# Two chunks of merge logits multiplied in the neighbourhood attention's block instead of the scan's

## The reference

```python
h = concatenate([h_ctx, h_lat])
(na_q, na_k, na_v, na_gate, pool_u, pool_gate, rw_r, rw_k, rw_v, rw_gate,
 rw_lw, rw_la, merge_logits) = split(h @ w_in, IN_SPLIT_POINTS)
y_na   = neighbourhood_attention(...)      # 16 heads of 64, softmax with bias and mask
y_pool = multiscale_pool(...)
y_rw   = rwkv_readout(... wkv_scan in both directions, 16 heads of 64 ...)
g_na, g_pool, g_rw = split(sigmoid(merge_logits), 3)
merged = g_na * (b_na @ w_branch[0]) + g_pool * (b_pool @ w_branch[1]) + g_rw * (b_rw @ w_branch[2])
out = merged @ w_out
```

## Time and profile before

| | us |
|---|---|
| median of 3 runs | 4159.89 |
| these runs | 4159.89, 4160.18, 4151.89 |
| the profiled execution, its own time | 4156.79 |
| its span | 4155.0 |
| TensorE busy in the span | 3791.7 (91%) |
| `att_h`, first to last matmul | 2657.3 to about 2811 |
| `feat`, first and last start of a dense product | 2818.7 and 3106.6 |
| `scan`, first to last start of a unit | 3121.4 to 3785.6 |
| `tail`, first start of a dense product to the span's end | 3797.6 to 4155.0 |

### The profile page before, as it was taken

How to read it: one execution, slowest core, us unless ns; L and a number is a source line. 1 busy time by engine, 2 the same in 40 slices (tenths; PEclk the granted TensorE clock), 3 DMA queues, 4 the chain that set the end, 5 groups by cost and what they waited for, 6 DMA issues and landing times. The chain is left out here.

```text
span 4155.0 us, 59251 instructions
## 1 busy us (share of the span) xinstructions
PE 3791.7 (91%) x25005; PEld 1903.5 (46%) x25005; DVE 1508.2 (36%) x2754; ACT 662.2 (16%) x1351; POOL 579.4 (14%) x840
## 2 busy tenths in 40 slices
PE   8899996899759999997999999898988899888998
PEld 1354443345424444453444444453435666664443
DVE  0499995372212214222100013243543334332411
ACT  0100001103230010231100000142441222221000
POOL 0001101111100001110000012341112323322100
PEclk9899998999979999998999999999999999999999
DMA  8788996872365456435545578636763334334662
GB/s 292 285 297 294 337 329 220 278 246 93 139 238 180 162 192 226 136 113 222 181 165 173 165 256 305 213 115 228 252 230 116 105 109 127 110 102 152 210 227 101
DMA packets 360590, 822.68 MB, mean 198 GB/s; under 512 B 27604, under 2 KB 63724, under 8 KB 353396
## 3 DMA queue, kind: packets, MB, share of 16 engines
q1 hardware_dynamic: 258524, 485.10, 35.1%
q0 software_dynamic: 73632, 275.55, 18.5%
q10 hardware_dynamic: 28172, 58.27, 3.7%
HBM read 698.02 MB, written 120.82 MB: 197 GB/s over the span
## 5 line engine op out<-in xcount | busy, mean ns | idle before, releaser
L1058 PE MATMUL gemm_a_g_ps<-store_w,turned 128*128 128x512 f32 (+1 forms) x1152 | 454.8, 557 | 2.4 <-PEq L205 2.4
L835 DVE SCALAR_TENSOR_TENSOR pmods_acc<-pmods_w,cond,pmods_acc 128x512 f32<-128x512 f32 x600 | 424.2, 748 | 23.9 <-issue 0.9
L1058 PE MATMUL out_c_g_ps<-store_w,turned 128*128 128x512 f32 (+1 forms) x1024 | 399.3, 552 | 0.0
L1058 PEld LDWEIGHTS gemm_a_g_ps<-store_w,turned 128*128 128x128 f32 x1152 | 208.5, 190 | 248.2 <-issue 248.2
L2305 PE MATMUL scan_g_ps<-store_w,turned 64*64 64x512 f32 x2048 | 295.4, 612 | 19.9 <-PEq L1441 14.2
L1058 PEld LDWEIGHTS out_c_g_ps<-store_w,turned 128*128 128x128 f32 x1024 | 184.5, 190 | 213.8 <-issue 213.8
L1058 PE MATMUL att_a_g_ps<-store_w,turned 128*128 128x512 f32 x512 | 238.3, 598 | 13.8 <-PEq L3130 9.9
L1058 PE MATMUL gemm_hq_g_ps<-store_w,turned 128*128 128x512 f32 x512 | 222.1, 597 | 7.4 <-PEq L3130 7.4
L1058 PE MATMUL out_a_g_ps<-store_w,turned 128*128 128x512 f32 x512 | 220.3, 592 | 1.1 <-PEq L205 1.1
L1058 PE MATMUL out_a_g_ps<-store_w,turned_c 128*128 128x512 f32 x512 | 220.2, 592 | 0.0
L1058 PE MATMUL feat_g_ps<-store_w,turned 128*128 128x512 f32 x384 | 182.6, 625 | 21.6 <-ACT feat_stage L1688 13.6
(11 more groups left out here) (439 smaller groups left out, 4983.6 us busy)
## 6 DMA issues: line engine op xcount, KB each, us to landing
store_w<-in_w_in SPq DMA_DIRECT2D x160, 1024.0 KB, 5.5
pmods_w<-in_w_mod POOLq DMA_DIRECT2D x40, 2048.0 KB, 11.4
store_w<-in_a_w_in SPq DMA_DIRECT2D x48, 1024.0 KB, 9.0
store_w<-in_c_w_in SPq DMA_DIRECT2D x48, 1024.0 KB, 5.2
mods_w<-in_w_mod SPq DMA_DIRECT2D x32, 1024.0 KB, 9.4
store_w<-in_a_w_out SPq DMA_DIRECT2D x32, 1024.0 KB, 5.0
scan_raw<-s_feat SPq DMA_DIRECT2D x112, 256.0 KB, 4.1
s_feat<-feat_o POOLq DMA_DIRECT2D x16, 1536.0 KB, 8.8
```

The lines of the kernel that those rows point to most:

```text
L835: v.scalar_tensor_tensor(a, src, x, a, ALU.mult, ALU.add)
L1058: mm = pe.matmul(to, lhs, self.store.slot[i % self.store.NS][:, k, :width], start=first, stop=last)
```

## The change

`merge_early` becomes chunks 0 to 3, and `merge_late` chunks 4 to 7, 10 and 11. Nothing else differs.

```diff
-        merge_early, merge_late, merge_last = merge_chunks(0, 2), merge_chunks(2, 8) + merge_chunks(10, 12), merge_chunks(8, 10)
+        merge_early, merge_late, merge_last = merge_chunks(0, 4), merge_chunks(4, 8) + merge_chunks(10, 12), merge_chunks(8, 10)
```

## The result

The changed kernel takes **4196.24 us** (median of 4 runs, 4193.17 to 4197.16) against 4160.03 of the kernel before beside it: a ratio of 1.0084, 95% interval 1.0068 to 1.0099. That is 36 us more and outside the predicted range. The profiled execution took 4196.41 us, with a span of 4194.6.

What follows compares the result with a forecast made beforehand. TensorE was taken to bound `att_h`, while scan stages wait for DVE, ACT or POOL, partly covered by units. `att_h` 47.5 us longer less scan 31 shorter gave +16.5 on 4156.8, stated as 4174 us; range 4162 to 4188.

Steps and rivals of the forecast that it cites:

- The evictions: `att_h`: four more evictions on ACT, each with two table loads, taken as 1 us for all.
- the 50 units priced at 0.88: `att_h`: new units standing where PE doesn't wait, 0.88 us each, 44.0 us longer.
- Rival 2: `att_h` has room: each unit costs 0.05 us, 3 us in all; change ends at -28, 4129. Chance 0.01.
- A: Scan: 12 units out behind half stages, 0.63 us each, 7.6 us back.
- B: Scan: 12 units out behind level stages, 0.37 us each, 4.4 us back.
- C: Scan: units behind stages ending in one short DVE or ACT operation, 0.60 us back each.
- D: Scan: units behind further stages ending in one short DVE or ACT operation, 0.60 us back each.
- E: Scan: 8 units out behind av of latent rounds, 0.87 us each, 7.0 us back.
- F: Scan: units behind other stages ending in one short DVE or ACT operation, 0.60 us each, 2.4 us back.
- G: Scan: 16 units at places where they hide entirely, 0.14 us each, 2.2 us back.
- rival 4: Scan: PE idler, time at 1.2 GHz doubles, 10 to 13 us lost; net +28, 4185. Chance 0.12.
- Rival 3: Scan: fewer matmuls mean fewer unexplained PE stalls, up to 10 us more back; net +6, 4163. Chance 0.18.

Runs made afterwards that it cites:

- none_at_halves: Changed kernel, but scan units placed as in the kernel before, less the 64 behind half1 to half5 and latent level5: 4179.32 us, ratio 1.0053.
- att_plus_two: Kernel before with chunks 2 and 3 multiplied a second time in `att_h`, its scan unchanged: 4221.75 us.
- scan_without_two: Kernel before with the products of chunks 2 and 3 left out of the scan, `att_h` as before: 4155.36 us in one run.
- none_between: Changed kernel, but scan units placed as in the kernel before, less the 64 behind turned, tz, outer, chain1 and y: 4171.75 us, ratio 1.0023.
- none_at_levels: Changed kernel, but scan units placed as in the kernel before, less the 64 behind level1 to level4 and context level5: 4185.48 us, ratio 1.0065.
- scan_one_chunk: Kernel before with only one of the scan's eight chunks multiplied, seven left out: 4042.34 us in one run.
- placed_192: Changed kernel with the scan's units placed by a table: two behind products, one behind av or rk and level1 to level4, rest spread: 4178.52 us, ratio 1.0042.
- placed_256: Kernel before with the scan's units placed by a table: two behind products, one behind av or rk and level1 to level4, rest spread: 4154.73 us, ratio 0.999.

## Why the prediction was wrong

**att_h: the total right, with luck.** 47.4 us for 47.5. The ten waits at L1982 are gone and the start-up wait shrank by 1.7, as forecast; that the block was bound by TensorE, read from starts without gaps, held. But two terms were off and cancelled. The evictions, for which I took 1 us, brought five waits of 4.2 us at L1996. That leaves 43.2 us for the 64 units, not 46.5: the 50 units priced at 0.88 cost about 0.81 each, as the step of 5.66 us for 4.04 shows. A row gives the distance to the next start, and another unit in the same step did not add the whole of it. Rival 2, room in `att_h`, is out: PE's weight loads are busy 52% there, and by the rule that was weighed the block would have had room; measured was 0.74 us a unit. Where there was room is below 64 units.

**scan: wrong, 6.7 us for 31.** Two steps failed. (`feat`, forecast unchanged within 3 us, was 3.8 shorter; nothing was tried there.)

The first is the group table, above all *A* and *B*. "12 x 0.63 = 7.6" and "12 x 0.37 = 4.4": the halves gave 2.0 and the levels 3.4 in the chain, together 5.4 for 12.0: the 0.37 that a bare level gives back is taken by the half behind it. The single prices were right (0.63 in none_at_halves, 0.37 at 3275.03). Wrong was to add them as if places were independent. I measured a stage from its start to the next stage's and did not ask what the next one then does. The sign of it stood in the earlier trace rows: the half behind the bare level has x16 and a wait for L2675 in front, where the others have x32 and no break. C and D, at 7.3 for 7.2, were right, and E, at 6.7 for 7.0, taken by itself. But F gave -1.3 for 2.4, and part of that is the same error. Of the chain stages chain1 lost 8 of its 16 units and gave back only 1.2 us: a chain1 of a context round with its unit takes 2.07 us where `outer` ahead of it has none, and 1.61 where it has one. And chain2 got 4 units more, for 3.0 us, which a price per unit of the group can't show. G gave 1.0 for 2.2, and the wait for L2766 grew as I said, to 5.0 us. In all the chain gave 19.2 us for 30.8.

The second is that I took every us of chain for a us of scan. 12 went into excess. Part of it goes with what rival 4 describes: time at half clock rose from 21 to 50 us (the rounded 0.98 had made me start from 27), and of the 14 us that half of that would be, some 8 show in places without a gap. Rival 3 took the stalls for something that fewer matmuls would lessen; they did not fall, 13 of 24.4 us before and 13 of 26.0 after. How much of the 12 us belongs to the change is open. The same scan in another kernel had 11 us more excess with 256 units (att_plus_two, 61.4 for 50.2) and 1 more with 192 (scan_without_two, 63.5 for 62.2), so that in the mean of both pairs 7 us went there. That shorter stages bring more of it is borne out by none_at_halves and none_between (68.8 and 70.1), not by none_at_levels (42.3) and scan_one_chunk (40.0); placed_192 and placed_256 say less, since 14.5 and 6.9 us of their growth are waits for DVE's addition. Gaps, clock and chance can't be parted further, since no run held the clock and changed the gaps, or the reverse.

**Sign, range, chances.** The forecast's sign held, and with it the reason: TensorE full in `att_h`, waits under the units in the scan. Its size did not: +36 for +14. The condition under which I called it wrong ("if the scan shrinks by under 20") was met. The range ended where rival 4's ended; rival 4 and the failed group sum together, 47.5 - 19 + 12 = 40, were in no case of mine. I had priced the bad cases one at a time.

## What to carry to other kernels

Before a filler's price is taken from two like stages, read on through the next stage: with two interleaved chains a filler behind one stage may only be using up the wait of the next. Price a removal over the pair, or over the round. And a unit that fills waits has its worth at a corner: in `att_h` the second 32 cost 0.10 us each and each one beyond them 0.74, while without any the engine's clock fell and the block took nearly as long as with 128.

A filler that can itself wait belongs where its wait is over: two units in a row behind `products` met an addition that DVE does later in its own order, and held up all of TensorE's work for up to 3.8 us.

Where a sum comes out to a tenth of a us, check its terms all the same: in `att_h` two errors of 3 us cancelled.

Where stages are made shorter, don't count on all of it: in six of the eight kernels with a shorter chain than before's and no more units, the changed one among them, 45 to 94% of what the chain gained was lost again to excess. With single profiles whose excess differs by up to 11 us for the same scan, that is a tendency and not a price.

## What I had not expected of the hardware

- TensorE stops in the middle of a run of short matmuls for 1.0 to 3.2 us from start to start, each time until 1.2 to 1.65 us after one of its instruction packets of 16 KB landed, 26 of 26 in two traces. The views call it "issue".
- Half of the stretches at 1.2 GHz in the changed scan (6 of 12) begin within 1.5 us of the end of such a gap of 1.8 to 2.5 us.
- Without its filling units `att_h` ran at 1.2 GHz for some 160 of its 195 us, though PE was busy in 76% of it (148.58 of 195).
- A unit on the whole array between 64x64 products costs 0.37 us more behind a level and 0.06 more behind a half than one on quadrants, with a quarter of its instructions. Why the two differ was not tried.
